# Five heads' expert queries and scores moved between the expert rows of the heads before them, and 26 cache copies paced by those rows

## The chip, the cores and the metric

One core of a Trainium2 chip runs the whole program. The metric is the device time of one execution in microseconds (us); lower is better. The kernel before was timed in three runs: 1211.47, 1214.36 and 1212.51 us, median 1212.51.

## What is computed

One inference step of one decoder layer, for a prompt of 256 tokens and 8 sample tokens with caches of 2048 positions. Width 1024, everything in float32. Cut to what matters:

```python
hp = rms_norm(xp, norm_mix) * (1 + sc1) + sh1             # adaLN: shifts, scales, gates from c @ w_ada
qa, ka, va, qb, kb, vb = project_qkv(hp, w_in)            # 8 stick-breaking heads, 8 dilated-window heads
xp = xp + g1 * merge_out(oa, ob, ...)                     # attention, out-projection, gated residual
...                                                       # the same for the samples, over cached pages and windows
def peer_ffn(h, w_pq, sub_keys, expert_u, expert_v):      # per token, 8 heads, top 16 of 16384 experts
    q = (h @ w_pq).reshape(t, 8, 2, 128)
    s = einsum('thcd,hcnd->thcn', q, sub_keys)            # 128 + 128 sub-key scores of a head
    s_top, i_top = top_k(s, 16)
    cand = s_top[:, :, 0, :, None] + s_top[:, :, 1, None, :]
    c_top, c_pos = top_k(cand, 16)                        # 16 experts of a token and head
    g = softmax(c_top)
    act = gelu(einsum('thkd,td->thk', expert_u[expert], h))
    return einsum('thk,thkd->td', g * act, expert_v[expert])
# outputs: y_prompt, y_sample, the new K/V rows, and the 8 samples' window buffers moved on by one row
```

The last of these outputs, `dil_k_s` and `dil_v_s`, are two caches of 8 x 2048 x 512 floats, copied from the inputs one row further on.

## The kernel before

**Stages.** The program is written out by hand, engine by engine, with semaphores: `sp` (SyncE) and `pool` (GpSimd) issue the transfers, `pe` the matmuls, `dve` and `act` the rest. It runs the adaLN and q/k/v projections, then attention over cached keys (`keys`), then over cached values, in turns b = 0 to 7, one for each sample (`pages_pv`, `window_pv`, mixed with the prompt's attention), the out-projection (`out_bank`), the expert queries and scores (`query_group`, `score_group`), and the expert rows.

**Value stage.** For each sample GpSimd gathers four quads of value pages (`value_quad`, 1 MB each, into slots 4, 5, 8, 9 of the tile `R`), each when the same quad of the sample before is used up (`v_used`). SyncE loads the window rows of the sample into `DV` (slots 6 and 7 of `R`), from the third sample on when `window_pv` of two samples earlier is done (`vd_used`). The last weights of the out-projection are loaded at b = 5.

**Copies.** The window buffers are copied in 64 pieces of 1 MB from device memory to device memory, all by SyncE, between its other work: 16 early, 4 at the third sample's window rows, 44 after the last sample's window rows, and these only after SyncE has waited for `v_used` 29 (the first quad of the last sample) and loaded the sub-keys. A piece waits for the one before it on its own semaphore, so that two are out at a time, and up to four where the semaphores change.

**Queries and scores.** Eight 1 MB weights go through slots 0 to 3 of `R`, the first four loaded as the last out-projection group frees the slots, the others as `query_group` frees them. For each head two query groups of 8 matmuls are followed by two small score groups. ScalarE moves the results out (`pq_ev`). VectorE picks the experts of a unit (one head of one half of the prompt tokens) with `choose`.

**Expert rows.** There are 16 units of 16 rows and 8 rows for the samples, 264 in all. `head_rows` on GpSimd gathers one row of 1 MB (the u and v vectors of one expert for each of 128 tokens) by an indirect transfer, 8 slots deep (`NSLOT`), each when TensorE has used the slot (`e_used`). VectorE takes the dot product (`dot_rows`), ScalarE makes gelu, weight and a diagonal matrix (`head_weights`), TensorE adds the row to the sum (`experts`). `choose` of the unit after next runs between the dots.

The two places in GpSimd's program and SyncE's that set when expert rows and copies may start are these:

```python
            sp.wait_ge(s["v_used"], (NB - 1) * VQ + 1)
            sp.dma_start(subk, A["subk"].rearrange("p (g n) -> p g n", g=16)).then_inc(s["subk_in"], 16)
            copy_windows(1, 0, range(2, 4))
            for pair, odd in ((1, 1), (2, 0), (2, 1), (3, 0), (3, 1)):
                copy_windows(pair, odd)
...
            weight_rounds(10, CHUNKS // WSLOTS)
            ...
            head_rows(0, 0, True)
```

Of the kernel before, what the change touches and what calls it, by code (L numbers as in the profile page):

```python
# [56 lines left out]
GATE1, SHIFT2, SCALE2, GATE2 = range(4)  # L57
LATE = 2
# [76 lines left out]
def build(nc, A):  # L135
    ctx = ExitStack()
    with ctx:
# [56 lines left out]
        W = [R[:, s, :].rearrange("p (c n) -> p c n", c=KC) for s in range(WSLOTS)]  # L194
# [8 lines left out]
        subk = R[:, WSLOTS, :].rearrange("p (g n) -> p g n", g=16)  # L203
# [24 lines left out]
        def row_slot(k):  # L228

            return (5, 6, 7, 0, 1, 2, 3, 4)[k % NSLOT]  # L230
# [84 lines left out]
        EVEN, ODD = range(0, CPB, 2), range(1, CPB, 2)  # L315

        @block.sync
        def _(sp):
# [12 lines left out]
            def copy_piece(pair, odd, m, q):  # L331


                src, dst = ((A["dil_k"], A["dil_k_s"]), (A["dil_v"], A["dil_v_s"]))[m]
                n = (PAST - 1) * DG // 4
                landed = copied[2 * odd + m]
                if not (isinstance(pair, int) and isinstance(q, int) and pair + q == 0):
                    sp.wait_ge(landed, pair * 64 + q * 16)
                sp.dma_start(dst[bass.ds(pair * 2 + odd, 1), bass.ds(q * n, n)].rearrange("a (r n) -> (a r) n", r=P),
                             src[bass.ds(pair * 2 + odd, 1), bass.ds(q * n + DG, n)].rearrange("a (r n) -> (a r) n", r=P)  # L340
                             ).then_inc(landed, 16)

            def copy_windows(pair, odd, quarters=range(4)):
                for q in quarters:
                    for m in range(2):
                        copy_piece(pair, odd, m, q)


# [3 lines left out]
            for odd in range(2):  # L352
                copy_windows(0, odd)
# [63 lines left out]
            for n in range(4):  # L417
                sp.wait_ge(copied[n], 16 * 4 * NB // 2)
# [4 lines left out]
        def _(pool):  # L423
# [40 lines left out]
            weight_rounds(10, CHUNKS // WSLOTS)  # L464

            def head_rows(i, par, first):
# [4 lines left out]
                for k in range(TOPK):  # L471
                    if first and row_slot(k) < WSLOTS:

                        pool.wait_ge(s["w_used"], CHUNKS - WSLOTS + row_slot(k) + 1)
                    elif first and row_slot(k) == WSLOTS:
                        pool.wait_ge(s["score_mm"], UNITS)
# [10 lines left out]
            with pool.Fori(1, NH) as i:  # L487
# [13 lines left out]
        def _(pe):  # L501
# [407 lines left out]
            pe.wait_ge(s["subk_in"], 16)  # L909
            base = ADA_CH + QKV_CH + OUT_CH  # L910

            def query_group(r, k, j, first):
                m = r * 8 + (2 * k + j)
                if j == 0:
                    w_round(base // WSLOTS + r, k)
                if not (first and 2 * k + j < 2):
                    pe.wait_ge(s["pq_ev"], m - 1)
                for c in range(KC):
                    last = pe.matmul(ps[:, j, 0:NTOK], W[k][:, c, j * P:(j + 1) * P], hT[:, c, :],  # L919
# [3 lines left out]
            def score_group(r, k, j, first):  # L923
                m = r * 8 + (2 * k + j)
                pe.wait_ge(s["pq_ev"], m + 1)
                if not (first and 2 * k + j < 2):
                    pe.wait_ge(s["score_ev"], m - 1)
                for t in range(2):
                    last = pe.matmul(ps[:, 2 + j, t * P:(t + 1) * P], eq[:, j, t * P:(t + 1) * P],
                                     subk[:, bass.ds(m, 1), :].rearrange("p a n -> p (a n)"), start=True, stop=True)  # L930
                last.then_inc(s["score_mm"], 1)

            def pq_round(r, first):
                for k in range(WSLOTS):
                    for j in range(2):
                        query_group(r, k, j, first)
                    for j in range(2):
                        score_group(r, k, j, first)

            pq_round(0, True)  # L940
            with pe.Fori(1, 2) as r:
                pq_round(r, False)

            pe.wait_ge(s["pq_ev"], 16)
            for j in range(2):
                for h in range(NH):
                    m = 2 * h + j
                    last = pe.matmul(ps[:, 0, j * NKEY:(j + 1) * NKEY], eqz[:, m * P:(m + 1) * P],
                                     subk[:, m, :], start=(h == 0), stop=(h == NH - 1))
            last.then_inc(s["score_mm"], 1)  # L950

            for k in range(QUADS):
                if k == 2:
                    pe.wait_ge(s["hr_mm"], 2)
                g = slice(k * QUAD, (k + 1) * QUAD)
                pe.matmul(ps[:, 6 + k % 2, (k // 2) * WC:(k // 2 + 1) * WC], cst("rep8")[g, :], H4[g, :], start=True, stop=True
                          ).then_inc(s["hr_mm"], 1)


            def experts(t, banks):  # L960
# [3 lines left out]
                with pe.Fori(0, NH) as h:  # L964
                    for k in range(TOPK):
                        pe.wait_ge(s["diag_done"], h * TOPK + (t * 128 + k + 1))
                        for q in range(2):
                            last = pe.matmul(ps[:, banks + q, :], diag[:, k % 4, :],  # L968
                                             R[:, row_slot(k), D + q * 512:D + (q + 1) * 512],
                                             start=False, stop=False, skip_group_check=True)  # L970
                        last.then_inc(s["e_used"], 1)
# [3 lines left out]
            experts(0, 4)  # L975
            pe.wait_ge(s["hr_ev"], 1)
            experts(1, 6)
# [14 lines left out]
        def _(act):  # L992
# [110 lines left out]
            def late_spread_ev(n):  # L1103
                spread_ev(n // 2, n % 2, n)
# [76 lines left out]
            def pq_ev(r, k, first):  # L1181
                for j in range(2):
                    m = r * 8 + (2 * k + j)

                    if j == 0:
                        act.wait_ge(s["pq_mm"], r * 4 + (k + 1))
                    else:
                        act.wait_ge(s["w_used"], r * 4 + (ADA_CH + QKV_CH + OUT_CH + k + 1))
                    if not (first and k == 0):
                        act.wait_ge(s["score_mm"], m - 1)  # L1190
                    h = r * 4 + k
                    act.activation(eqz4[:, :, m, h * NB:(h + 1) * NB],
                                   ps[:, j, SEQ:NTOK].rearrange("p (a n) -> p a n", a=1).to_broadcast([P, 2, NB]), ACT.Copy)
                    act.activation(eq[:, j, 0:SEQ], ps[:, j, 0:SEQ], ACT.Copy).then_inc(s["pq_ev"], 1)
                for j in range(2):
                    m = r * 8 + (2 * k + j)
                    h = r * 4 + k
                    act.wait_ge(s["score_mm"], m + 1)
                    act.activation(S[:, bass.ds(h, 2, step=NH), j, :],
                                   ps[:, 2 + j, 0:256].rearrange("p (t n) -> p t n", t=2), ACT.Copy  # L1200
                                   ).then_inc(s["score_ev"], 1)


# [3 lines left out]

            act.wait_ge(s["z_v"], 1)
            for k in range(WSLOTS):
                pq_ev(0, k, True)  # L1210
                if k == 2:
                    top_exp(0)
            for k in range(WSLOTS):
                pq_ev(1, k, False)
                if k == 1:
                    top_exp(1)
            act.wait_ge(s["score_mm"], 17)
            act.activation(S[:, UNITS - 1, :, :], ps[:, 0, 0:2 * NKEY].rearrange("p (c n) -> p c n", c=2),
                           ACT.Copy).then_inc(s["score_ev"], 1)
            act.wait_ge(s["hr_mm"], 4)  # L1220
            for b in range(2):
# [685 lines left out]
```

## Time and profile before

| what | value |
|---|---|
| median of 3 runs | 1212.51 us |
| the profiled execution | 1215.47 us, its span 1213.8 us |
| TensorE busy | 909.9 us (75%) |
| VectorE busy | 635.5 us (52%) |
| GpSimd busy | 420.2 us (35%) |
| ScalarE busy | 351.8 us (29%) |
| moved by DMA | 481.21 MB, mean 396 GB/s |
| mean granted TensorE clock | 0.907 |

The profile covers one execution; times inside it are counted from the span's start. The busy shares are means over stages that differ, so that a stage is read from the stretches of it. The chain of waits follows the work that ended last back to what released it. The rows of the 16 DMA engines give a busy share (1.00 is all of them busy) and what they moved.

### The profile page before, as it was taken

How to read it: one execution, taken by the hardware profiler on the slowest of the kernel's cores; microseconds unless marked ns; L12 is line 12 of the kernel's file. 1: busy time of each engine (PE TensorE's matmuls, PEld its weight loads, DVE VectorE, ACT ScalarE, POOL GpSimd, SP SyncE). 2: the span in 40 equal slices, each digit the busy share in tenths (PEclk: the TensorE clock that was granted, in tenths of full speed). 3: DMA queues.
4: the chain of work that ended last, by engine and by line, in shares of the span. 5: the costliest groups of instructions: out<-in, count | busy, mean ns of one | idle time of the engine just before them, and what ended most of it. 6: DMA issues, size and time to landing. Idle time of an engine off the chain costs nothing.

```text
span 1213.8 us, 13371 instructions
## 1 busy us (share of the span) xinstructions
PE 909.9 (75%) x3662; PEld 423.6 (35%) x3662; DVE 635.5 (52%) x1604; ACT 351.8 (29%) x959; POOL 420.2 (35%) x430
## 2 busy tenths in 40 slices
PE   2797986668676879964778877877587777777783
PEld 0342443445232448831323322333233322323231
DVE  4200106553222544223776777777777777777755
ACT  0000001463121012221333233323433444244323
POOL 1201323112231000211455554545454455555551
PEclk9799988777898889977999999999999999999996
DMA  9999999988999899999999999999989999999996
GB/s 366 424 379 400 378 365 364 397 338 351 373 392 413 281 367 378 388 396 393 410 414 428 420 428 427 428 428 428 428 357 427 428 427 428 428 428 428 427 427 272
DMA packets 72826, 481.21 MB, mean 396 GB/s; under 512 B 9953, under 2 KB 10306, under 8 KB 27346
## 3 DMA queue, kind: packets, MB, share of 16 engines
q0 software_dynamic: 54720, 377.53, 76.0%
q1 hardware_dynamic: 18066, 103.17, 22.1%
q8 instruction: 22, 0.36, 0.1%
q14 instruction: 18, 0.15, 0.0%
HBM read 477.41 MB, written 70.32 MB: 451 GB/s over the span
## 4 chain that ended last, share of the span: by engine, by line
DMA 46%; PE 30%; issue 8%; DVE 8%; ACT 3%; POOL 2%; SPq 2%; POOLq 0%; DVEq 0%; ACTq 0%
DMA R<-in_uv,idst 29%; PE ps L968 11%; DMA out_dil_v_s<-in_dil_v 6%; DMA R<-in_sb_v,vrow 5%; PE ps L919 5%; PE ps L874 2%; PE ps L576 2%; POOL R L480 2%; DMA R<-in_sb_k 2%; DVE R L1770 2%; DMA vrow<-in_vrow 2%; PE ps L739 2%; PE ps L602 1%; DMA R<-in_uv,idec 1%; ACT wgt L1241 1%
## 5 line engine op out<-in xcount | busy, mean ns | idle before, releaser
L968 PE MATMUL ps<-R,diag 128*128 128x512 f32 x1024 | 491.9, 630 | 168.8 <-ACT diag L1260 167.3
L480 POOL DMA_INDIRECT R<-in_uv,idst x256 | 313.7, 1225 | 365.6 <-PE ps L968 294.6
L1770 DVE CUSTOM_DVE_ANT_0 R<-R,H 128x1024 f32<-128x1024 f32 x264 | 319.3, 1224 | 201.7 <-DMA R<-in_uv,idst 190.7
L968 PEld LDWEIGHTS ps<-R,diag 128*128 128x128 f32 x1024 | 195.7, 199 | 465.0 <-ACT diag L1260 252.0
L1238 ACT ACTIVATE gel<-dots 128x2 f32<-128x2 f32 x132 | 26.8, 203 | 403.9 <-DVE dots L1770 403.9
L576 PE MATMUL ps<-R,HT 128*128 128x512 f32 x192 | 94.3, 631 | 3.9 <-DMA R<-in_wts 3.9
L1260 ACT ACTIVATE diag<-const,wgt 128x128 f32<-128x128 f32 x256 | 88.9, 394 | 14.7 <-PE ps L968 1.4
L310 POOL DMA_INDIRECT R<-in_sb_v,vrow x32 | 30.4, 951 | 114.5 <-PE ps L739 90.2
L432 POOL DMA_DIRECT2D R<-in_wts x24 | 12.8, 541 | 157.3 <-PE ps L874 57.2
L301 POOL DMA_DIRECT2D R<-in_sb_k x64 | 34.7, 542 | 86.5 <-issue 85.9
L1241 ACT ACTIVATE wgt<-gel,gst 128x1 f32<-128x1 f32 x264 | 63.3, 287 | 4.3
L919 PE MATMUL ps<-HT,R 128*128 128x264 f32 x256 | 60.6, 397 | 0.7 <-ACT HT L999 0.7
L739 PE MATMUL ps<-R,ast 128*32 128x512 f32 x256 | 38.7, 678 | 24.2 <-DMA R<-in_sb_v,vrow 23.7
L602 PE MATMUL ps<-R,Z 128*32 128x256 f32 x512 | 37.2, 408 | 22.9 <-DMA R<-in_sb_k 22.9
L576 PEld LDWEIGHTS ps<-R,HT 128*128 128x128 f32 x192 | 36.6, 200 | 47.6 <-issue 43.0
L919 PEld LDWEIGHTS ps<-HT,R 128*128 128x128 f32 x256 | 49.5, 196 | 9.6 <-ACT HT L999 1.1
L514 PE MATMUL ps<-R,cT 128*32 128x256 f32 x384 | 33.5, 505 | 18.4 <-DMA R<-in_wts 18.4
L1402 DVE TENSOR_TENSOR m_all<-m_all,R 128x1536 f32<-128x1536 f32 x6 | 10.5, 1754 | 56.8 <-DMA m_all<-out_dil_k_s 56.8
L1015 ACT ACTIVATE QKV<-ps 128x512 f32<-128x512 f32 x12 | 6.9, 597 | 86.8 <-PE ps L576 86.8
L602 PEld LDWEIGHTS ps<-R,Z 128*32 128x32 f32 x512 | 13.8, 113 | 50.3 <-DMA R<-in_sb_k 28.1
L874 PE MATMUL ps<-R,HT 128*128 128x512 f32 x64 | 30.7, 636 | 0.8 <-DVE HT L1625 0.8
L1238 ACT ACT_TABLE_LOAD x24 | 30.8, 1283 | 1.0
(282 smaller groups left out, 828.6 us busy)
## 6 DMA issues: line engine op xcount, KB each, us to landing
R<-in_wts POOLq DMA_DIRECT2D x48, 1024.0 KB, 17.0
out_dil_k_s<-in_dil_k SPq DMA_DIRECT2D x32, 1023.5 KB
out_dil_v_s<-in_dil_v SPq DMA_DIRECT2D x32, 1023.5 KB
R<-in_sb_k SPq DMA_DIRECT2D x64, 256.0 KB, 8.3
R<-in_sb_k POOLq DMA_DIRECT2D x64, 256.0 KB, 6.7
R<-in_win_v SPq DMA_DIRECT2D x8, 512.0 KB
R<-in_uv,idst POOLq DMA_INDIRECT x256, 11.8
m_all<-in_win_k SPq DMA_DIRECT2D x6, 512.0 KB
```

Source lines behind the costliest of these rows:

```text
L301: eng.dma_start(KV[c % KVS][:, g, :], cache[bass.ds(page, 1)].rearrange("a p n -> (a p) n")).then_inc(ready[c % KVS], 16)
L480: pool.indirect_dma_start(out=R[:, row_slot(k), :], out_offset=None, in_=A["uv"], in_offset=bass.IndirectOffsetOnAxis(ap=idst[:, par, k:k ...
L576: last = pe.matmul(ps[:, n, :], hT[:, 2 * k + c, t * P:(t + 1) * P], WA[k][:, c, half * 512:(half + 1) * 512], start=(k + c == 0), stop=(2 ...
L602: last = pe.matmul(ps[c * QUAD:(c + 1) * QUAD, bank, at:at + WC], qz[:, half, c, b, :], KV[cc][:, :, c * P:(c + 1) * P], start=(b == 0 and ...
L739: last = pe.matmul(quad(0, u), ast[:, i % 2, 4 * m + u, :], R[:, VS[m], u * DG:(u + 1) * DG], start=(m == 0), stop=(m == VQ - 1))
L874: last = pe.matmul(ps[:, n, :], hT[:, c, t * P:(t + 1) * P], WA[c // 2][:, c % 2, half * 512:(half + 1) * 512], start=(c == 0), stop=(c == ...
L919: last = pe.matmul(ps[:, j, 0:NTOK], W[k][:, c, j * P:(j + 1) * P], hT[:, c, :], start=(c == 0), stop=(c == KC - 1))
L968: last = pe.matmul(ps[:, banks + q, :], diag[:, k % 4, :], R[:, row_slot(k), D + q * 512:D + (q + 1) * 512], start=False, stop=False, skip ...
L1238: act.activation(gel[:, k:k + 2], dots[:, k:k + 2], ACT.Gelu_apprx_tanh).then_inc(s["gel_done"], 1)
L1241: last = act.activation(wgt[:, k + q:k + q + 1], gel[:, k + q:k + q + 1], ACT.Copy, scale=gst[:, k + q:k + q + 1])
L1260: act.activation(diag[:, k % 4, :], ident, ACT.Copy, scale=wgt[:, k:k + 1]).then_inc(s["diag_done"], 1)
L1770: dve.tensor_tensor_reduce(u, u, H[:, t, :], 1.0, 0.0, ALU.mult, ALU.add, dots[:, k:k + 1]).then_inc(s["dot_done"], 1)
```

## The change

Eight pieces of it act together:

- The slots of `R` for the query weights become 5, 6, 7, 8, 9, 8, 9, 8 for heads 1 to 8 (`WQ`). The first four are loaded by GpSimd once the value pages and window rows in those slots are used up, the fifth when the first head's queries are done, the last three ahead of the rows of units 3, 4 and 5.
- The sub-keys move from slot 4 of `R` to the rows of `m_all` that held GATE1 and SCALE2 (`ROW` puts these two beside each other), and are loaded by GpSimd when the second norm is done (`h_ready` 6).
- TensorE works out queries and scores of heads 1 to 3 as before. Those of head h + 4 (h = 0 to 4) are put after rows 1, 5, 9 and 11 of unit h (`next_head`), the samples' scores after row 1 of unit 5 and their rows after row 5. ScalarE's parts stand after rows 3, 7, 11 and 15.
- Expert row k goes to slot k (modulo 8) of `R`, which is free of query weights from the start.
- `top_exp` of the first two units stands after the scores of heads 2 and 3 (it stood after those of heads 3 and 6).
- The 64 copies are one numbered row, two out at a time: 16 early (`EARLY`), 4 at the third sample (`GAP` 20), 18 after the last sample's window rows (`PACED` 38), with no other wait than that for the copy two before.
- The last 26 are issued one for every 4 expert rows that TensorE has used (`PACE` 4).
- The final norm's weights are loaded before these 26.

```diff
+ROW = (0, 2, 1, 3)
+COPIES = 8 * NB
+EARLY, GAP, PACED, PACE = 16, 20, 38, 4
...
-        W = [R[:, s, :].rearrange("p (c n) -> p c n", c=KC) for s in range(WSLOTS)]
+        WQ = [R[:, s, :].rearrange("p (c n) -> p c n", c=KC) for s in (5, 6, 7, 8, 9, 8, 9, 8)]
...
-        subk = R[:, WSLOTS, :].rearrange("p (g n) -> p g n", g=16)
+        subk = m_flat[:, 0:2 * D].rearrange("p (g n) -> p g n", g=16)
...
-            return (5, 6, 7, 0, 1, 2, 3, 4)[k % NSLOT]
+            return k % NSLOT
...
+            def copies(first, end, ahead, pace=0):
+
+                for n in range(first, end):
+                    if n >= ahead:
+                        sp.wait_ge(copied[(n - ahead) % 4], 16 * ((n - ahead) // 4 + 1))
+                    if pace:
+                        sp.wait_ge(s["e_used"], (n - first) * pace + 1)
...
-            for odd in range(2):
-                copy_windows(0, odd)
+            copies(0, EARLY, 2)
...
-                    copy_windows(1, 0, range(2))
+                    copies(EARLY, GAP, 2)
...
-            sp.wait_ge(s["v_used"], (NB - 1) * VQ + 1)
-            sp.dma_start(subk, A["subk"].rearrange("p (g n) -> p g n", g=16)).then_inc(s["subk_in"], 16)
-            copy_windows(1, 0, range(2, 4))
-            for pair, odd in ((1, 1), (2, 0), (2, 1), (3, 0), (3, 1)):
-                copy_windows(pair, odd)
-
+            copies(GAP, PACED, 2)
             sp.wait_ge(s["h_ready"], 6)
-            sp.dma_start(m_all[:, SHIFT2, :], A["norm_final"].to_broadcast([P, D])).then_inc(s["fin_in"], 16)
+            sp.dma_start(m_all[:, ROW[SHIFT2], :], A["norm_final"].to_broadcast([P, D])).then_inc(s["fin_in"], 16)
+            copies(PACED, COPIES, 2, PACE)
...
-            weight_rounds(10, CHUNKS // WSLOTS)
+            def query_weight(h, slot):
+                pool.dma_start(R[:, slot, :], A["wts"][QUERIES + h]).then_inc(w_ready[h % WSLOTS], 16)
+
+            pool.wait_ge(s["v_used"], (NB - 1) * VQ + 2)
+            query_weight(0, 5)
+            for h in range(1, 3):
+                pool.wait_ge(s["vd_used"], NB - 2 + h)
+                query_weight(h, 5 + h)
+            pool.wait_ge(s["v_used"], (NB - 1) * VQ + 3)
+            query_weight(3, 8)
+            pool.wait_ge(s["h_ready"], 6)
+            pool.dma_start(subk, A["subk"].rearrange("p (g n) -> p g n", g=16)).then_inc(s["subk_in"], 16)
+            pool.wait_ge(s["w_used"], QUERIES + 1)
+            query_weight(4, 9)
...
+            for i in range(2, 5):
+                pool.wait_ge(s["w_used"], QUERIES + i + 2)
+                query_weight(i + 3, 8 + i % 2)
+                head_rows(i, i % 2, False)
...
+            def next_head(h):
+
+                return {1: lambda: query_group(h, 0), 5: lambda: query_group(h, 1),
+                        9: lambda: score_group(h, 0), 11: lambda: score_group(h, 1)}
...
-            experts(0, 4)
+            clear(0, 4)
+            for h in range(NH):
+                experts_beside(h, next_head(h + 3) if h < 5 else {1: decode_scores, 5: decode_rows} if h == 5 else {})
...
+            for h in range(3):
+                for j in range(2):
+                    query_ev(h, j)
+                for j in range(2):
+                    score_ev(h, j)
+                if h:
+                    top_exp(h - 1)
```

**SyncE, after the last sample's window rows.** `in_win_v` are window rows, `in_dil` and `out_dil` the copies. Before:

```order
L281 DMA R<-in_win_v 128x1024 [waits vd_used]
L283 DMA R<-in_win_v 64x512
L287 DMA R<-out_dil_v_s 1x512
L401 DMA R<-in_subk 128x2048 [waits v_used]
L339 DMA out_dil_k_s<-in_dil_k 16x16376 [waits copied0]
L339 DMA out_dil_v_s<-in_dil_v 16x16376 [waits copied1]
```

and with the change:

```order
L284 DMA R<-in_win_v 128x1024 [waits vd_used]
L286 DMA R<-in_win_v 64x512
L290 DMA R<-out_dil_v_s 1x512
L345 DMA out_dil_k_s<-in_dil_k 16x16376 [waits copied2]
L345 DMA out_dil_v_s<-in_dil_v 16x16376 [waits copied3]
...
L400 DMA m_all<-in_norm_final 128x1024 [waits h_ready]
L345 DMA out_dil_k_s<-in_dil_k 16x16376 [waits e_used,copied0]
L345 DMA out_dil_v_s<-in_dil_v 16x16376 [waits e_used,copied1]
```

The wait for `v_used` and the sub-keys no longer stand between the window rows and the copies.

**GpSimd, from the last value quads to the first expert rows.** `in_sb_v` are value pages, `in_wts` weights, `in_uv` expert rows. Before:

```order
L310 DMA R<-in_sb_v,vrow 128x2048 [waits v_used] x8
L428 UNCONDITIONAL_BRANCH
...
L432 DMA R<-in_wts 128x2048
L431 REGISTER_ALU
L432 ISA [waits w_used]
...
L468 COPY idst<-idx 128x16 [waits top_done]
L480 DMA R<-in_uv,idst 128x2048 [waits id_st,c_in]
L480 DMA R<-in_uv,idst 128x2048 x2
L480 DMA R<-in_uv,idst 128x2048 [waits w_used] x4
L480 DMA R<-in_uv,idst 128x2048 [waits score_mm]
```

and with the change:

```order
L313 DMA R<-in_sb_v,vrow 128x2048 [waits v_used] x8
L459 DMA R<-in_wts 128x2048 [waits v_used]
L459 DMA R<-in_wts 128x2048 [waits vd_used] x2
L459 DMA R<-in_wts 128x2048 [waits v_used]
L469 DMA m_all<-in_subk 128x2048 [waits h_ready]
L459 DMA R<-in_wts 128x2048 [waits w_used]
L475 COPY idst<-idx 128x16 [waits top_done]
L486 DMA R<-in_uv,idst 128x2048 [waits w_used,id_st,c_in]
L486 DMA R<-in_uv,idst 128x2048 [waits w_used] x3
L486 DMA R<-in_uv,idst 128x2048
L486 DMA R<-in_uv,idst 128x2048 [waits w_used] x3
```

Five weights and the sub-keys stand ahead of the first expert row, where eight weights stood, the last of which waited for the queries of head 4.

## Rows read from the trace of the kernel before

**Rows 1.** Stretches: length, engines' busy us, PEclk, DMA share, GB/s.
```profile
400.00:436.00 36.00, 34.06 (x146) 17.64 (x147) 17.61 (x34) 1.49 (x4) 0.00 (x0) 0.86 0.89 303
487.00:557.00 70.00, 50.35 (x217) 36.49 (x215) 13.46 (x39) 12.39 (x40) 12.19 (x12) 0.88 0.99 389
590.00:869.00 279.00, 213.99 (x455) 85.17 (x456) 205.81 (x543) 99.53 (x313) 142.19 (x122) 0.98 1.01 424
880.00:890.00 10.00, 10.00 (x19) 4.30 (x18) 8.86 (x31) 4.24 (x15) 3.99 (x4) 0.76 0.63 249
```
**Rows 2.** Chain of waits in order of time: start, us, what.
```profile
390.19 1.07 PE ps L739 x8
...
447.61 1.98 PE ps L530 x8
...
450.26 9.62 PE ps L919 x32
...
460.41 0.71 PE ps L929 x4
461.12 7.14 PE ps L919 x32
...
654.90 12.31 DMA R<-in_uv,idst
...
1189.39 14.01 DMA R<-in_uv,idec
```
**Rows 3.** SyncE's issues in order of time.
```profile
361.65 0.35 SPq L281 DMA_DIRECT2D R<-in_win_v  x1
...
387.05 0.35 SPq L401 DMA_DIRECT2D R<-in_subk  x1
387.44 0.81 SPq L339 DMA_DIRECT2D out_dil_k_s<-in_dil_k  x1
...
488.91 0.51 SPq L339 DMA_DIRECT2D out_dil_k_s<-in_dil_k  x1
...
556.31 0.51 SPq L339 DMA_DIRECT2D out_dil_v_s<-in_dil_v  x1
```
**Rows 4.** GpSimd in order of time.
```profile
477.28 0.53 POOL L432 DMA_DIRECT2D R<-in_wts  x1 [7.85 <-PE ps L919]
485.67 0.53 POOL L432 DMA_DIRECT2D R<-in_wts  x1 [7.86 <-PE ps L919]
487.18 1.00 POOL L480 DMA_INDIRECT R<-in_uv,idst  x1 [0.78 <-POOL idst L468]
```
**Rows 5.** VectorE in order of time, the first `choose`.
```profile
461.58 0.29 DVE L1719 COPY QKV<-QKV 128x256 f32<-128x256 f32 x1 [14.03 <-ACT QKV L1199]
...
472.41 0.17 DVE L1754 CAST idx<-QKV 128x16 int32<-128x16 f32 x1
479.87 0.17 DVE L1756 TENSOR_REDUCE QKV<-QKV 128x1 f32<-128x16 f32 x1 [7.28 <-ACT QKV L1206]
```
**Rows 6.** DMA queues 361 to 375 us: packets, MB, share of 16 engines.
```profile
q1 hardware_dynamic: 226, 0.66, 14.1%
```
**Rows 7.** DMA queues 375 to 390 us.
```profile
q0 software_dynamic: 789, 5.68, 91.6%
```
**Rows 8.** DMA queues 487 to 557 us.
```profile
q1 hardware_dynamic: 546, 17.43, 60.8%
q0 software_dynamic: 1349, 9.80, 38.2%
```
**Rows 9.** DMA queues 40 to 108 us.
```profile
q0 software_dynamic: 1616, 11.01, 42.1%
```
**Rows 10.** Packets 400 to 436 us, copies alone.
```profile
DMA packets 334, 10.90 MB, mean 303 GB/s; under 512 B 166, under 2 KB 166, under 8 KB 166
```
**Rows 11.** Stretch 450 to 460 us, columns as in rows 1.
```profile
450.00:460.00 10.00, 9.74 (x35) 8.01 (x36) 0.00 (x0) 0.77 (x5) 0.00 (x0) 0.76 1.17 468
```
**Rows 12.** The page's costliest groups: busy us, mean ns, idle before, releaser.
```profile
L968 PE MATMUL ps<-R,diag 128*128 128x512 f32 x1024 | 491.9, 630 | 168.8 <-ACT diag L1260 167.3
```

More of the change, by code:

```diff
@@ L315, in build @@
         EVEN, ODD = range(0, CPB, 2), range(1, CPB, 2)
+        QUERIES = ADA_CH + QKV_CH + OUT_CH
         @block.sync
@@ L471, in head_rows @@
                 for k in range(TOPK):
[L472 to L476, printed above, removed]
+                    if first and k < WSLOTS:
+                        pool.wait_ge(s["w_used"], QUERIES - WSLOTS + k + 1)
+                    elif first and WSLOTS < k < NSLOT:
+                        pool.wait_ge(s["w_used"], QUERIES + k - WSLOTS)
                     if not (first and k < NSLOT):
@@ L929, in score_group @@
                     last = pe.matmul(ps[:, 2 + j, t * P:(t + 1) * P], eq[:, j, t * P:(t + 1) * P],
-                                     subk[:, bass.ds(m, 1), :].rearrange("p a n -> p (a n)"), start=True, stop=True)
+                                     subk[:, m, :], start=True, stop=True)
                 last.then_inc(s["score_mm"], 1)
[L933 to L957, printed above, removed]
@@ L960, in experts, with decode_scores, decode_rows @@
-            def experts(t, banks):
+            def decode_scores():
+                pe.wait_ge(s["pq_ev"], 16)
+                for j in range(2):
+                    for h in range(NH):
+                        m = 2 * h + j
+                        last = pe.matmul(ps[:, 0, j * NKEY:(j + 1) * NKEY], eqz[:, m * P:(m + 1) * P],
+                                         subk[:, m, :], start=(h == 0), stop=(h == NH - 1))
+                last.then_inc(s["score_mm"], 1)
+            def decode_rows():
+                for k in range(QUADS):
+                    if k == 2:
+                        pe.wait_ge(s["hr_mm"], 2)
+                    g = slice(k * QUAD, (k + 1) * QUAD)
+                    pe.matmul(ps[:, 6 + k % 2, (k // 2) * WC:(k // 2 + 1) * WC], cst("rep8")[g, :], H4[g, :], start=True, stop=True
+                              ).then_inc(s["hr_mm"], 1)
@@ L961, in experts, with clear @@
+            for h in range(3):
+                for j in range(2):
+                    query_group(h, j)
+                if h == 0:
+                    pe.wait_ge(s["subk_in"], 16)
+                for j in range(2):
+                    score_group(h, j)
+            def clear(t, banks):
                 for q in range(2):
@@ L963, in experts, with expert, experts_beside @@
                               skip_group_check=True)
[L964 to L971, printed above, removed]
+            def expert(k, done, banks):
+                pe.wait_ge(s["diag_done"], done)
+                for q in range(2):
+                    last = pe.matmul(ps[:, banks + q, :], diag[:, k % 4, :],
+                                     R[:, row_slot(k), D + q * 512:D + (q + 1) * 512],
+                                     start=False, stop=False, skip_group_check=True)
+                last.then_inc(s["e_used"], 1)
+            def experts_beside(h, beside):
+                for k in range(TOPK):
+                    expert(k, h * TOPK + k + 1, 4)
+                    if k in beside:
+                        beside[k]()
+            def next_head(h):
+                return {1: lambda: query_group(h, 0), 5: lambda: query_group(h, 1),
+                        9: lambda: score_group(h, 0), 11: lambda: score_group(h, 1)}
             zeroP = tw[:, 2048:2048 + P]
             pe.wait_ge(s["z_v"], 1)
-            experts(0, 4)
+            clear(0, 4)
+            for h in range(NH):
+                experts_beside(h, next_head(h + 3) if h < 5 else {1: decode_scores, 5: decode_rows} if h == 5 else {})
             pe.wait_ge(s["hr_ev"], 1)
-            experts(1, 6)
+            clear(1, 6)
+            with pe.Fori(0, NH) as h:
+                for k in range(TOPK):
+                    expert(k, h * TOPK + (P + k + 1), 6)
             pe.wait_ge(s["score_ev"], UNITS)
@@ L1178, in _, with query_ev, score_ev @@
                 half_turned(1, half, (2, 5)[half], s["hT_ev"])
[L1181 to L1201, printed above, removed]
+            def query_ev(h, j):
+                m = 2 * h + j
+                if j == 0:
+                    act.wait_ge(s["pq_mm"], h + 1)
+                else:
+                    act.wait_ge(s["w_used"], QUERIES + h + 1)
+                if m >= 2:
+                    act.wait_ge(s["score_mm"], m - 1)
+                act.activation(eqz4[:, :, m, h * NB:(h + 1) * NB],
+                               ps[:, j, SEQ:NTOK].rearrange("p (a n) -> p a n", a=1).to_broadcast([P, 2, NB]), ACT.Copy)
+                act.activation(eq[:, j, 0:SEQ], ps[:, j, 0:SEQ], ACT.Copy).then_inc(s["pq_ev"], 1)
+            def score_ev(h, j):
+                m = 2 * h + j
+                act.wait_ge(s["score_mm"], m + 1)
+                act.activation(S[:, bass.ds(h, 2, step=NH), j, :],
+                               ps[:, 2 + j, 0:256].rearrange("p (t n) -> p t n", t=2), ACT.Copy
+                               ).then_inc(s["score_ev"], 1)
             def top_exp(i):
@@ L1261, in head_weights @@
                                        ).then_inc(s["diag_done"], 1)
+                    if beside and k in beside:
+                        beside[k]()
                     if top is not None and k == 13:
@@ L1265, in head_weights @@
                         final_root(1)
-            head_weights(0, first=True, top=2)
-            with act.Fori(1, NH) as h:
-                head_weights(h, top=h + 2)
+            for h in range(NH):
+                head_weights(h, first=(h == 0), top=h + 2,
+                             beside=next_head(h + 3) if h < 5 else {3: decode_score_ev, 7: decode_rows_ev} if h == 5 else None)
             final_root(0)
@@ L1800, in _ @@
                 all_of(choose(i, scores=2 * i + 2))
-            with dve.Fori(0, NH) as h:
+            with dve.Fori(0, NH - 2) as h:
+                dot_rows(h, 0, beside=choose(h + 2, scores=2 * h + 6))
+            with dve.Fori(NH - 2, NH) as h:
                 dot_rows(h, 0, beside=choose(h + 2))
-            all_of(finish(0, 4, s["e_used"], NH * TOPK, m_all[:, GATE2, :]))
+            all_of(finish(0, 4, s["e_used"], NH * TOPK, m_all[:, ROW[GATE2], :]))
             with dve.Fori(0, NH - 1) as h:
```

88 lines of the change are left out of this document (40 added, 48 removed).

## The prediction

> **What bounds the kernel now.** I read the stretches first. In the expert rows the 16 DMA engines are full: a share of 1.01 at 424 GB/s from 590 to 869 us [rows 1], so a gathered row of 1.0486 MB costs 2.473 us. There are 264 of them, 652.9 us. TensorE, at 75% busy, is not the limit there: a row is two pairs of its matmuls at 0.63 us [rows 12], 1.26 us. Before the rows, the chain of waits shows a stretch bound by nothing but computation: the last quad of value pages is used at 390.19, and from there out-projection, norm, queries (from 450.26) and the first `choose` follow each other [rows 2]. Little of this stretch needs data, and what fills the DMA engines meanwhile is the copies: alone they reach 303 GB/s at a share of 0.89 [rows 1]. So the time is the DMA engines' work plus their idle time, and I ask of each edit what it does to that idle time. The profiled execution took 1215.47 us (span 1213.8), 3.0 above the median of 1212.51; I add differences to the median.
>
> **Term 1, the first expert row is issued earlier.** Before, GpSimd issues it at 487.18, because it first waits until 485.67 for the last weight's slot; and the first unit is complete only at 480.6, since VectorE waits for ScalarE's exponential, 7.28 us [rows 4, 5]. With the change the index is there at 472.6, the exponential follows the scores of head 2 (a head takes 8.4 us, 7.14 of it queries [rows 2]; so about 470), and the unit is done at about 473.4. From the unit to the issue are 1.1 us more (a copy of the index and the 0.78 behind it [rows 4]): 474.5. That is 12.7 us earlier, provided that the chain before it stands still. Slot 7 waits for head 3's queries, at 476.7, which is in time.
>
> **Term 2, what the DMA engines still have to do then.** Before, 18 copies are issued from 488.91 to 556.31 [rows 3] and about one of the two under way is left: 19. From 487.2 to the last landing at 1203.4 (1189.39 + 14.01 [rows 2]) are 716.2 us. Less 652.9 of rows, 4.1 of a stall at 880 to 890 (249 GB/s where 424 would flow [rows 1]), 1.2 for the final norm's weights (0.52 MB) and 4.1 for some 1.7 query weights in flight (of those issued at 477.28 and 485.67 [rows 4]), 53.9 us are left, 2.84 per copy. Now 26 copies and 3 weights stand behind that point: 7 more copies, +19.9 us; weights +3.3; the final norm's weights are moved ahead, -1.2; the engines start empty, +1. Terms 1 and 2 together: -12.7 + 23.0 = **+10.3 us**. Bounds for a copy: 2.24 us, its 1.0486 MB at 468 GB/s, the highest of the stretches of 10 us or more [rows 11], and 3.46 alone (1.0486 over 303 GB/s). A share of 26 would then cost -15.6 or +16.1.
>
> **Term 3, the 18 copies start in front of the last value pages.** SyncE has issued the last window rows by 363 us, and then waits 24 us for the first quad of the last sample; only then come the sub-keys and the copies, at 387.44 [rows 3]. The change has no wait there. The window rows fill SyncE's ring up to about 375 (0.66 MB of q1 from 361 to 375 [rows 6]), so the copies get going at 375. From there to 390, q0 still has to bring 5.68 MB, the last value pages [rows 7], and these are what the chain waits for. How q0 fares beside copies, two stretches tell: it gets 9.80 MB in 70 us, 0.140 MB/us, while q1 moves 17.43 [rows 8], and 11.01 MB in 68 us, 0.162 [rows 9]. At 0.140 the 5.68 MB take 40.6 us instead of 15: the last value page lands some **25 us** later, and everything behind it, the first expert row too, moves by that. Nothing is won back: by 416 some ten copies are done, the other eight and four weights fill the engines to about 447, and they then stand empty for about 50 us, until the first expert rows at 499.5, but for sub-keys, one weight and the final norm (2.6 MB). Bounds: half of 389 GB/s for q0 gives 29 us, a delay of 14; 0.162 gives 20. At the other end q0 waits altogether. Its packets are small, 9.80 MB in 1349 [rows 8], some 8 kB; those of a copy are large: of 334 packets while copies ran alone 166 are under 512 B, and the other 168 carry 10.90 MB, 65 kB each [rows 10].
>
> The Trainium skill (DMA: Bandwidth & Descriptors, section Queues, rings and completion order) says that a DMA engine goes round its queues packet by packet. With these packets that would leave q0 one byte in nine and make the delay of this term 48 us in place of 25; the rows give q0 36% of the bytes [rows 8], so that the trace does not agree, and the measured share decides.
>
> **What costs nothing.** Five heads' queries on TensorE, 7.9 us each, 39 in all, stand between rows that come every 2.47 us or slower: 16 rows take 20.2 us of TensorE, with the queries 28.1, of at least 39.6. A group of 3.6 us holds up slots while a gather takes 12 us to land [rows 2], so that some five remain under way; without this cover it would cost up to 39 us. ScalarE's extra moves replace the same ones earlier. SyncE's paced copies hold nothing behind them but the y stores. Sub-keys: issued when the norm is done (before 447.61 [rows 2]), 12 us ahead of the first scores, 1 MB on engines by then empty; if copies still ran, up to 8 us of wait. Weights 5 to 8 are asked for nine rows ahead. The early copies no longer go four deep where the semaphores change: 0, within 3 us either way.
>
> **Sum.** +10.3 + 25 = +35 us: 1212.5 + 35.3 = **1248 us**. With a delay of 14 to 30 it is 1237 to 1253. A measurement tells this kernel from no change by about 0.2%, 2.4 us.
>
> **Rivals.**
> *No delay.* The value pages keep their rate beside the copies. For: they are 4 to 6 gathers deep, deeper than the weights of rows 9. Against: rows 8 hold up to 8 gathers in flight, and q0 still fell to 0.140. Then +10.3, about 1223; sub-keys late behind copies add up to 8. Chance 0.12.
> *Large packets first.* q0 gets one packet of 8 kB for each of 65, a ninth of 389 GB/s, 0.043 MB/us. The 18 copies (18.9 MB) are through at 430, q0 has 2.4 MB by then and the other 3.3 take some 8 us: a delay of 48, +58, 1270 us. For: the sizes [rows 10]. Against: the 36% of rows 8. Chance 0.06. The Trainium skill's rule, told under term 3, is this case.
> *Paced copies nearly free, faster.* One copy among eight gathers leaves no gap between packets, and the value pages are not held up either. It decides when a copy costs under 2.35 us: 10.3 - 26 x 0.49 = -2.4. At 2.24 [rows 11] it is -5.3, 1207 us. The work stays the same, so that idle time is the most it can win: 4.0 us from 400 to 436 (0.11 of 36) and the stall of 4.1 [rows 1], 1204 us. For: there are stretches above the 424 GB/s of the rows alone [rows 1, 11]. Against: they are short, beside others that are lower, and 389 is the mean over 70 us. Chance 0.14.
> *It moves nothing.* A delay near 0, copies near 2.47 us (their bytes at 424 GB/s, -9.6) cancel terms 1 and 2; also if SyncE reached the copies late, which rows 3 speak against. 1213. Chance 0.10.
> The forecast has 0.58. Slower: 0.58 + 0.12 + 0.06 = 0.76. The range of 1212 to 1262 leaves out the faster case and the large packets, 0.20.
>
> **What the new profile would show.** SyncE's first copy after the window rows at about 363; the last value quad used near 415 and not 390; queries of head 1 from about 475; DMA share falling far below 0.5 between 447 and 499; then 26 copies one for every 4 rows, last near row 101, and a period near 3.2 us per row; no idle of the expert rows behind the queries. It would be wrong if the last value quad still lands near 390, or if rows with copies between them come faster than 3.0 us each, or if TensorE's queries starve the gathers.

## Result: 3% slower, and the profile of the changed kernel

The changed kernel takes 1247.85 us (median of 4 runs, 1244.09 to 1251.91) against 1212.5 (4 runs, 1211.47 to 1214.36): a ratio of 1.029, 95% interval 1.0255 to 1.0325. The forecast was 1248. Its profiled execution took 1251.91 us, with a span of 1250.2.

The stretches of the changed kernel, columns as in [rows 1]:

```profile
390.00:416.00 26.00, 13.88 (x62) 5.79 (x62) 5.95 (x22) 2.41 (x7) 2.06 (x3) 0.64 1.00 391
416.00:436.00 20.00, 10.61 (x56) 4.88 (x56) 4.95 (x15) 3.45 (x5) 1.06 (x2) 0.70 1.01 401
436.00:450.00 14.00, 11.90 (x34) 6.39 (x34) 7.16 (x14) 0.04 (x1) 0.00 (x0) 0.76 0.88 346
450.00:475.00 25.00, 25.00 (x124) 11.96 (x123) 10.41 (x20) 1.49 (x4) 0.00 (x0) 1.00 0.00 1
475.00:500.00 25.00, 18.16 (x73) 14.44 (x72) 9.25 (x27) 3.99 (x14) 1.06 (x2) 0.80 0.30 105
500.00:520.00 20.00, 14.25 (x66) 11.06 (x65) 17.54 (x75) 4.73 (x15) 7.83 (x9) 0.92 0.46 180
...
528.00:860.00 332.00, 264.31 (x670) 129.97 (x669) 190.92 (x495) 98.62 (x323) 124.43 (x118) 0.90 1.01 425
```

From 450 to 475 us, where 25 us of TensorE work stand in 25 us, the DMA engines move nothing (share 0.00), and from 475 to 520 less than half of what they can. In the kernel before, this time was full of copies:

```profile
450.00:475.00 25.00, 24.53 (x106) 20.57 (x107) 9.50 (x41) 4.00 (x15) 1.06 (x2) 0.90 1.00 384
475.00:500.00 25.00, 24.69 (x121) 21.03 (x120) 10.02 (x44) 6.50 (x20) 5.16 (x7) 1.00 1.06 431
```

With the change the copies are gone too early, as SyncE's issues show (to be held against [rows 3]):

```profile
365.37 0.35 SPq L284 DMA_DIRECT2D R<-in_win_v  x1
...
367.66 0.54 SPq L345 DMA_DIRECT2D out_dil_k_s<-in_dil_k  x1
...
440.73 0.51 SPq L345 DMA_DIRECT2D out_dil_v_s<-in_dil_v  x1
482.56 0.36 SPq L400 DMA_DIRECT2D m_all<-in_norm_final  x1
528.69 0.51 SPq L345 DMA_DIRECT2D out_dil_k_s<-in_dil_k  x1
```

The 18 copies run from 367.66 to about 448, and the next is issued at 528.69, with the first expert row used. The last value pages suffer beside them. TensorE in order of time (the idle time before a row and its releaser in brackets), to be held against 390.19 in [rows 2]:

```profile
412.06 1.93 PE L750 MATMUL ps<-R,ast 128*32 128x512 f32 x8 [6.05 <-DMA R<-in_sb_v,vrow]
...
419.79 1.93 PE L750 MATMUL ps<-R,ast 128*32 128x512 f32 x8 [4.94 <-DMA R<-in_sb_v,vrow]
425.00 1.93 PE L750 MATMUL ps<-R,ast 128*32 128x512 f32 x8 [3.28 <-DMA R<-in_sb_v,vrow]
...
485.25 9.47 PE L927 MATMUL ps<-HT,R 128*128 128x264 f32 x32 [0.69 <-ACT HT L1022]
```

The last quad comes at 425.00 and not 390.19; the queries start 60.2 us behind it (60.1 before). These 8 matmuls take 1.93 us and not 1.07: TensorE waited for half of this time, and its granted clock, a mean between its levels of 1.2 and 2.4 GHz, is down to 0.64 until 416 us and 0.70 until 436; for the last quad that costs 0.9 us on the path. The first expert row, GpSimd and VectorE (compare [rows 4, 5]):

```profile
507.75 0.23 DVE L1790 TENSOR_SCALAR gall<-QKV 128x16 f32<-128x16 f32 x1
508.05 0.20 POOL L475 COPY idst<-idx 128x16 int32<-128x16 int32 x1 [12.51 <-DVE gall L1790]
509.01 1.00 POOL L486 DMA_INDIRECT R<-in_uv,idst  x1 [0.77 <-issue]
...
529.39 0.94 POOL L486 DMA_INDIRECT R<-in_uv,idst  x1 [10.62 <-PE ps L974]
```

The balance of the two profiled executions, in us against the kernel before:

| part | predicted | measured | from |
|---|---|---|---|
| window rows issued | 0, within 3 | +3.7 | 365.37 against 361.65 |
| window rows to last quad | +25 | +31.1 | 59.6 against 28.5 |
| last quad to queries | 0 | +0.2 | 60.25 against 60.07 |
| queries to first row | -12.7 | -13.2 | 23.76 against 36.92 |
| first row to last | +23.0 | +14.2 | 730.4 (509.01 to 1239.40) against 716.2 |
| end | 0 | +0.4 | 10.8 against 10.4 |
| sum of the span | +35.3 | +36.4 | 1250.2 against 1213.8 |

The last landing is the last row's issue and the 13.2 us that it takes to land (14.0 before). The 26 copies beside the rows are issued from 528.69 to 840.20, one for every 4 rows, so that a row takes 3.1 us there, near the 3.2 forecast.

### The profile page after: what moved, and what is told of

The parts are those of the page before. It is cut to its first block and busy times, and to the rows that moved or that the text cites. A ratio compares the mean times of both kernels' runs of the same rounds, so it can differ in the third digit from the quotient of the medians.

```text
span 1250.2 us, 13002 instructions
## 1 busy us (share of the span) xinstructions
PE 932.9 (75%) x3662; PEld 435.7 (35%) x3662; DVE 636.6 (51%) x1604; ACT 350.6 (28%) x959; POOL 408.1 (33%) x431
## 5 line engine op out<-in xcount | busy, mean ns | idle before, releaser
L974 PE MATMUL ps<-R,diag 128*128 128x512 f32 x1024 | 507.9, 648 | 158.9 <-ACT diag L1288 158.9
L486 POOL DMA_INDIRECT R<-in_uv,idst x256 | 299.1, 1168 | 393.3 <-PE ps L974 349.3
L974 PEld LDWEIGHTS ps<-R,diag 128*128 128x128 f32 x1024 | 204.5, 207 | 448.7 <-ACT diag L1288 225.3
L750 PE MATMUL ps<-R,ast 128*32 128x512 f32 x256 | 42.6, 742 | 45.0 <-DMA R<-in_sb_v,vrow 44.5
L927 PEld LDWEIGHTS ps<-HT,R 128*128 128x128 f32 x256 | 49.9, 196 | 14.2 <-issue 5.0
L1565 DVE TENSOR_TENSOR msk<-ps,const 128x512 f32<-128x512 f32 x8 | 5.5, 691 | 64.5 <-PE ps L750 64.5
L613 PEld LDWEIGHTS ps<-R,Z 128*32 128x32 f32 x512 | 14.0, 115 | 54.4 <-DMA R<-in_sb_k 30.4
L885 PE MATMUL ps<-R,HT 128*128 128x512 f32 x64 | 30.4, 631 | 0.8 <-DVE HT L1655 0.8
```

The costliest lines, as they stand in the source:

```text
L486: pool.indirect_dma_start(out=R[:, row_slot(k), :], out_offset=None, in_=A["uv"], in_offset=bass.IndirectOffsetOnAxis(ap=idst[:, par, k:k ...
L613: last = pe.matmul(ps[c * QUAD:(c + 1) * QUAD, bank, at:at + WC], qz[:, half, c, b, :], KV[cc][:, :, c * P:(c + 1) * P], start=(b == 0 and ...
L750: last = pe.matmul(quad(0, u), ast[:, i % 2, 4 * m + u, :], R[:, VS[m], u * DG:(u + 1) * DG], start=(m == 0), stop=(m == VQ - 1))
L927: last = pe.matmul(ps[:, j, 0:NTOK], WQ[h][:, c, j * P:(j + 1) * P], hT[:, c, :], start=(c == 0), stop=(c == KC - 1))
L974: last = pe.matmul(ps[:, banks + q, :], diag[:, k % 4, :], R[:, row_slot(k), D + q * 512:D + (q + 1) * 512], start=False, stop=False, skip ...
```

## The experiments

All run times are against the kernel before on the same chip; its median there was 1209.63 us for the first four, 1210.99 for the second four and 1208.80 for the last four. Where I compare kernels timed in different groups, or the change with any of these, I go by the ratios; a hundredth is 12.1 us. The moment at which SyncE issues the last window rows varied between 355 and 368 us from one profiled execution to the next, with the same program up to there. So I give the last quad as its distance D from that issue: 28.5 us in the kernel before, 59.6 with the change. Each D comes from one profiled execution. In the lines of DMA queues, q0 carries GpSimd's transfers (the gathers and the query weights) and q1 SyncE's (the copies).

**e1_guard: SyncE's wait put back.**

```diff
+            sp.wait_ge(s["v_used"], (NB - 1) * VQ + 1)
             copies(GAP, PACED, 2)
```

> The change, with SyncE's wait for the first quad of the last sample (v_used 29) put back ahead of the 18 copies. My theory (the copies in front of the last value pages cost 31 us, everything else some 5): the last quad is used near 394 us in place of 425, the first expert row is issued near 478, the span falls from 1250 to about 1219, 1215 to 1222 us by the clock, 1.002 to 1.008 of the kernel before. Rival (the queries beside the expert rows, or the 26 paced copies, are what costs): still 1240 or more.

Measured: 1215.68 us, ratio 1.0055 (1.003 to 1.008). D is 26.2. Putting this one line back takes away 28 us of the 35 (0.0235 by the ratios), and the rival, that the queries or the paced copies between the rows are what costs, is refuted: it had 1240 or more. GpSimd issues the first row at 468.77, 110.2 us behind the last window rows (125.5 before); yet the kernel is still 0.5% slower, because the copies end at about 450 again before the first row:

```profile
400.00:436.00 36.00, 35.03 (x142) 16.37 (x142) 13.95 (x28) 1.63 (x5) 0.00 (x0) 0.93 0.99 374
436.00:450.00 14.00, 7.63 (x23) 5.81 (x24) 6.07 (x11) 1.75 (x6) 0.53 (x1) 0.63 0.82 301
450.00:460.00 10.00, 9.90 (x49) 8.44 (x48) 3.06 (x15) 2.13 (x8) 0.53 (x1) 1.00 0.45 162
460.00:475.00 15.00, 14.03 (x65) 10.88 (x64) 12.88 (x57) 4.38 (x12) 4.97 (x6) 1.00 0.30 100
```

**e2_before_early: the copies alone moved, in the kernel before.**

```diff
+            copy_windows(1, 0, range(2, 4))
+            copy_windows(1, 1)
+            copy_windows(2, 0, range(3))
             sp.wait_ge(s["v_used"], (NB - 1) * VQ + 1)
             sp.dma_start(subk, ...)
-            copy_windows(1, 0, range(2, 4))
-            for pair, odd in ((1, 1), (2, 0), (2, 1), (3, 0), (3, 1)):
+            copy_windows(2, 0, range(3, 4))
+            for pair, odd in ((2, 1), (3, 0), (3, 1)):
                 copy_windows(pair, odd)
```

> The kernel before, with 18 of its copies issued ahead of the wait for v_used 29 (and of the sub-keys), as in the change; 26 are left behind it. My theory (a late value page costs nothing as long as copies fill the engines while the computation behind it runs): the last quad is used 20 to 30 us later than 390, near 415 to 425, and yet the time stays within 6 us of the kernel before, 1210 to 1219 us. Rival (the delay itself is the price): 1238 or more.

Measured: 1220.56 us, ratio 1.0101 (1.0068 to 1.0134), 1.6 us above the range. D is 66.1, 37.6 more than before, and the first expert row is issued at 522.21 and not 487.18; of these 35 us only 11 arrive in the time. The late value pages are thus not the price as such; while copies fill the engines they cost little. But the copies are used up at 530, and then the engines run at 0.85 to 0.88, since the first rows wait for slots that the queries free one every 8.4 us:

```profile
500.00:560.00 60.00, 59.18 (x304) 50.30 (x303) 23.07 (x86) 13.54 (x46) 9.43 (x12) 1.00 0.88 344
560.00:600.00 40.00, 32.24 (x68) 12.76 (x67) 25.39 (x68) 16.16 (x48) 18.37 (x17) 0.96 0.85 338
```

0.12 of 60 and 0.15 of 40 are 13 us of idle time. D is also 6.5 us more than in the change, though the same 18 copies stand in front: here they go up to four deep where the semaphores change, and q0 gets only 0.124 MB/us (372 to 422 us):

```profile
q1 hardware_dynamic: 415, 13.56, 69.0%
q0 software_dynamic: 856, 6.20, 32.6%
```

**e3_all_paced: no copies in the gap.** `EARLY, GAP, PACED, PACE = 16, 20, 20, 4`

> The change with PACED 20: no copies after the last window rows, 44 paced by the expert rows. My theory (the loss is idle engines between the last value page and the first expert row): the last quad is used near 394 us and the first row issued near 478, as with the wait put back, but the engines stand idle for some 65 us in between and 18 copies more, 2.47 us each, stand beside the rows: span about 1264, 1257 to 1268 us. Rival (what matters is that no copy stands in front of the value pages): about 1217.

Measured: 1256.61 us, ratio 1.0383 (1.0324 to 1.0442), 0.4 under the range, and 11 us slower than the change by the ratios, although the last quad comes in time again (D 27.3).

```profile
400.00:440.00 40.00, 36.31 (x148) 17.19 (x146) 17.63 (x35) 1.69 (x5) 0.00 (x0) 0.92 0.00 1
440.00:478.00 38.00, 31.65 (x134) 25.21 (x134) 20.92 (x86) 8.52 (x27) 7.11 (x10) 0.87 0.34 124
```

65 us idle (40, and 0.66 of 38). Value pages in time are thus not enough; copies must also fill what comes behind them. The rows also price a paced copy: first row to last takes 774.1 us here and 732.4 in e1_guard, 41.7 for 18 copies, 2.32 each.

**e4_guard_unpaced: the wait put back, no pacing.** `copies(PACED, COPIES, 2)`

> As e1_guard, but the last 26 copies are issued two deep without waiting for expert rows. Theory A (a copy costs its bytes, 2.47 us, only if it runs singly beside deep gathers; two deep it costs 2.84): 26 x 0.37 = 9.6 us slower than e1_guard. Theory B (the work of the engines is the same however it is spaced): within 3 us of e1_guard. Theory C (copies that start right behind the norm fill the engines before the first expert row): up to 10 us faster than e1_guard.

Measured: 1214.71 us, ratio 1.0025 (0.9994 to 1.0056): 1 us under e1_guard by the medians and 3.6 by the ratios, whose intervals overlap, as theory B has it. But theory A's 9.6 us and C's 10 may also cancel. Five of the unpaced copies are issued before the first expert row (459.19 to 475.80, against 478.23), and four copies moved ahead of the rows save 9.7 us in e5_guard_42 below, so that something of C is there and something has to stand against it. The profiled execution took 1223.57 us, 9 over the median, so I take no price of a copy from it, and this stays open.

**e5_guard_42 and e6_guard_44: more copies in the gap.** As e1_guard with `PACED` 42 and 44.

> As e1_guard, with PACED 42: 22 copies after the last window rows and 22 beside the expert rows. In e1_guard the engines had a share of only 0.3 to 0.45 between 450 and 475 us. My theory (only idle time of the engines counts): four copies move from beside the rows, at about 2.4 us each, into that gap: 9 to 10 us faster than e1_guard, 0.995 to 0.999 of the kernel before. Rival (copies that reach past the norm hold up sub-keys and the first rows): no faster than e1_guard.

> As e1_guard, with PACED 44: two more copies than e5_guard_42 ahead of the rows. My theory: the gap is full with four, so that these two run against sub-keys and first rows: within 3 us of e5_guard_42 either way. Rival (the later the copies end, the better, as in the kernel before, where they ended at 565 us): another 5 us faster.

Measured: 1208.99 us, ratio 0.9975 (0.9954 to 0.9996), and **1199.86 us, ratio 0.9904 (0.9875 to 0.9932)**. The first is as expected, 9.7 us under e1_guard by the ratios; the second is another 9 us better by medians and ratios, 6.5 by the two spans (1209.2 and 1202.7), where I had expected nothing: the gap was not full with 22 copies. First row to last takes 732.4, 724.1 and 719.6 us with 26, 22 and 20 copies beside the rows, 2.1 us less for each. In e5_guard_42, then in e6_guard_44:

```profile
460.00:475.00 15.00, 14.85 (x74) 12.81 (x75) 11.37 (x51) 4.40 (x12) 1.08 (x3) 1.00 0.64 246
```

```profile
460.00:475.00 15.00, 14.89 (x73) 12.66 (x71) 12.70 (x59) 3.94 (x12) 2.41 (x4) 1.00 0.87 311
```

0.36 of 15 us were still idle, room for two copies.

**e7_one_deep: the change, its 18 copies one at a time, no wait.** `copies(GAP, PACED, 1)`

> The change (no wait put back), with the 18 copies one at a time. My theory (the value pages lose bandwidth to SyncE's queue in the measure in which it always has a copy ready): q0 gets more than the 0.135 MB/us it had beside two copies, the last quad is used near 410 and not 425 us, and the copies reach further into the gap: 1225 to 1238 us, 10 to 22 faster than the change. Rival (one copy under way takes as much from q0 as two): last quad near 425, and 1244 to 1250 us.

Measured: 1223.62 us, ratio 1.0111 (1.0069 to 1.0153), 22 us faster than the change by the ratios, and 1.4 us under the range. D is 38.5: the delay falls from 31 to 10 us, more than I had expected. DMA queues of this kernel from 369.4 to 392.7 us, from the issue of one copy to that of the third behind it, then of the change from 385 to 420:

```profile
q0 software_dynamic: 938, 6.83, 69.5%
q1 hardware_dynamic: 96, 3.14, 31.3%
```

```profile
q1 hardware_dynamic: 283, 9.17, 63.5%
q0 software_dynamic: 702, 5.10, 40.2%
```

The value pages get 0.293 MB/us beside one copy and 0.146 beside two.

**e8_small_packets: the change, with 8 kB packets in the 18 copies.** `[:, 0:width]` on both sides of them, width 2046 of 2047; the last element of each of their rows is left out.

> The change, with the 18 copies cut so that their packets are 8 kB (128 rows of 2046 elements) and not 65 kB; the last element of each row of 2047 of these 18 is left out. Theory A (an engine goes round its queues packet by packet, so that packets of one size share evenly): q0 gets about half, 0.19 MB/us, from 375 us on, the last quad is used near 408, some 15 us faster than the change. Theory B (the share comes from something else, the size of a packet does not matter): q0 keeps 0.13 to 0.15 MB/us, last quad near 425, time within 4 us of the change.

Measured: 1241.27 us, ratio 1.0222 (1.0177 to 1.0267), 8 us faster than the change by the ratios where I had expected 15; with 4 runs of each the intervals still touch. D is 51.2, a delay of 23 and not 31. From 385 to 415 us:

```profile
q0 software_dynamic: 735, 5.33, 51.4%
q1 hardware_dynamic: 739, 5.39, 49.7%
```

735 packets against 739: with packets of one size the two queues take turns, as theory A has it, and share evenly. Theory B, that the size does not matter, is refuted: it had D unchanged. The value pages gain less than an even share promised, because the engines move less in all: 358 GB/s here (391 above). Such copies are slower alone, too: 254 GB/s from 436 to 466 us, against 303 [rows 1].

**e9_queries_twice: e6_guard_44 with the moved query matmuls done twice.**

```diff
-                for c in range(KC):
+                for c in list(range(KC)) * (2 if h > 2 else 1):
```

> As e6_guard_44, with the 8 matmuls of each query group of heads 4 to 8 done twice over (the second time gives the same result): 10 groups of 3.57 us more on TensorE between the expert rows. My theory (TensorE is covered beside rows that come every 2.5 us or slower): within 3 us of e6_guard_44, 1198 to 1204 us. Rival (work between rows holds up the slots and with them the gathers): up to 35.7 us more, 1215 to 1235.

Measured: 1219.11 us, ratio 1.0076 (1.0042 to 1.0109), 21 us above e6_guard_44 by the ratios: within the rival's range and not mine. First row to last is only 12.1 us longer (731.7 and 719.6), but the profiled execution was one of the fastest here and the slowest of its kernel in e6_guard_44. So of 35.7 us more matmuls between a third and three fifths shows. From 560 to 600 us, in e6_guard_44 and then here:

```profile
560.00:600.00 40.00, 27.79 (x70) 13.88 (x70) 23.53 (x59) 13.31 (x43) 13.96 (x14) 0.87 1.01 428
```

```profile
560.00:600.00 40.00, 32.38 (x97) 17.98 (x96) 21.26 (x57) 12.03 (x38) 14.30 (x14) 0.91 0.96 396
```

The queries once over leave the engines full (1.01), twice over they do not. The change itself has 1.01 from 528 to 860 us (above). So "hidden" held for the change, with less to spare than I had thought.

**e10_guard_46 and e11_guard_50: still more copies in the gap.**

> As e6_guard_44, with PACED 46. In e6_guard_44 the engines still had a share of 0.87 from 460 to 487 us, 3.5 us of idle time. My theory (a copy ahead of the rows saves its 2.4 us only as far as there is idle time): 0 to 4 us faster than e6_guard_44. Rival (first rows are held up by copies still running): 1 to 5 us slower.

> As e6_guard_44, with PACED 50: the last unpaced copies run beside the first expert rows, as in the kernel before. My theory: nothing left to win, within 4 us of e10_guard_46 either way, since the engines are full in both. Rival (two copies deep starve the first gathers, whose slots come back late): 5 us or more slower than e10_guard_46.

Measured: 1204.74 us, ratio 0.9963 (0.9939 to 0.9988), and 1205.91, ratio 0.9972 (0.995 to 0.9995). They are slower than e6_guard_44 by 7 and 8 us, so the rival of the first holds: beyond 24 copies, the last ones run beside the first rows. First row to last is 724.0 and 723.9 us, 4.4 more than in e6_guard_44. In e10_guard_46 VectorE waits 7.20 us for the second gathered row:

```profile
483.58 1.23 DVE L1801 CUSTOM_DVE_ANT_0 R<-R,H 128x1024 f32<-128x1024 f32 x1 [2.76 <-DMA R<-in_uv,idst]
492.01 1.23 DVE L1801 CUSTOM_DVE_ANT_0 R<-R,H 128x1024 f32<-128x1024 f32 x1 [7.20 <-DMA R<-in_uv,idst]
```

In e6_guard_44 these two are at 482.77 and 484.97, with a wait of 0.96. GpSimd issues the ninth row 30.4 us behind the first and not 21.4, and half of these 9 us comes back by the last row, as two copies fewer stand beside the later ones. Why e11_guard_50, whose second row comes in time, ends up the same is not shown.

**e12_two_late: e6_guard_44, the last two copies put into the stall at row 128.**

```diff
-                        sp.wait_ge(s["e_used"], (n - first) * pace + 1)
+                        sp.wait_ge(s["e_used"], (n - first) * pace + 1 if n < COPIES - 2 else NH * TOPK)
```

> As e6_guard_44, with the last two of the paced copies held back until expert row 128 is used, when VectorE ends the first half of the tokens and the gathers run dry (share 0.65 in ten us of e6_guard_44, some 4 us idle). My theory (only idle time counts, wherever it stands): the two copies, about 5 us of the engines' work, fill that stall: 2 to 4 us faster than e6_guard_44. Rival (the copies hold up the gathers that VectorE waits for at that point): no faster, or slower by up to 3 us.

Measured: **1197.81 us, ratio 0.9892 (0.9866 to 0.9918)**, the fastest of all, 1% under the kernel before. The same ten us in e6_guard_44 and then here:

```profile
870.00:880.00 10.00, 10.00 (x22) 4.26 (x21) 8.52 (x24) 3.02 (x11) 5.60 (x5) 0.88 0.65 257
```

```profile
870.00:880.00 10.00, 10.00 (x22) 4.38 (x21) 5.67 (x16) 2.66 (x10) 4.40 (x4) 0.87 1.02 426
```

The stall is filled: from 820 to 940 us the engines move 427 GB/s and not 408. First row to last falls from 719.6 to 715.5 us, as expected; by the ratios alone, 1.5 us apart, e12_two_late and e6_guard_44 can't be told apart (their intervals overlap).

## Why the prediction was right

The mechanism was the forecast one: SyncE's copies, which nothing held back any more, ran in front of the last value pages, moved the whole chain behind them, and were missing where that chain left the engines empty. e1_guard shows that the moved copies cost the time, e3_all_paced and e2_before_early that what is missing behind them is part of it. That the number fell within 1 us of the measured one is in part luck; two terms were off in opposite directions.

- **Term 1** (-12.7): measured -13.2, by the same steps.
- **Term 2** (+23.0): measured +14.2. What was mis-sized is mainly the copy. I took 2.84 us from a stretch in which copies run two deep beside few gathers; paced, beside eight gathers, q1 took 18.0% of 352 us for 27.25 MB, 2.44 us per copy, and the engines kept 425 GB/s. The term with 2.44 for the 26 is 9.4 + 3.3 - 1.2, and 2.6 for the start (19 us at 367 GB/s), 14.1.
- **Term 3** (+25): measured +31.1. The rate beside two copies was right (0.146 MB/us, predicted 0.140), but I let the copies start at 375; the first two land at 379.04 and 381.96, when SyncE issues the next, so that they had been moving since about 370. From 365 to 375 us q1 moved 1.57 MB, where the window rows alone were 0.66 [rows 6]. In the first 14 us from the window rows' issue q0 got 0.92 MB less than before. First the kernel before (361 to 375), then the change (365 to 379):

```profile
q0 software_dynamic: 607, 4.42, 87.5%
```

```profile
q0 software_dynamic: 485, 3.50, 60.7%
```

  At 0.146 MB/us these 0.92 MB are an estimated 6.3 us, the 6.1 that the term lacked. The window rows did not hold the copies up so long as I had them do.
- **The rule on queues.** Under term 3 I weighed the Trainium skill (DMA: Bandwidth & Descriptors, section Queues, rings and completion order), a round by packets. With packets of one size, and if a packet of the rule is one of those that the profile counts, e8_small_packets agrees to within 1% (735 and 739). With copies of 65 kB packets the one-for-one reading would have given a delay of 48 us, and 31 were measured. A likely reason, argued and not tested alone: a copy is only one such packet per engine, so with one or two under way an engine often has none of them waiting. It fits this that the delay falls from 31 to 10 us with one copy at a time, and grows to 37.6 with up to four (e2_before_early).
- **What costs nothing.** The queries cost nothing that shows, once over. The early copies too: the 3.7 us by which the profiled execution was late before 365 us lie within the 13 us by which this moment varies between runs of the same code.

## What to carry to other kernels

Where DMA bounds a kernel, ask of every change what the engines do between the last load that the computation waits for and the first load that it brings forth: background transfers are worth what they fill there, and starting them earlier loses twice, once for the loads they overtake and once for the gap they leave. Tie such transfers to an event at both ends (here `v_used` 29 and the number of copies), size them by the idle share of that stretch, and put what is left into any later stall. A wait that looks like it only protects a buffer may also be what keeps the background work in its place.

## What the runs showed of the hardware

What a gather queue keeps beside 1 MB copies depends on how many of them are under way: 0.293 MB/us beside one, 0.146 beside two, 0.124 beside up to four, and beside two copies cut to its own packet size half (5.33 MB of 10.72 in 30 us), packet for packet. Copies from device memory to device memory with 8 kB packets reach 254 GB/s alone, with 65 kB packets 303 [rows 1]. Spread among deep gathers, a copy costs no more than its bytes (2.1 to 2.4 us per MB), and copies and gathers together run at the gathers' own 425 GB/s.
